# Sparse attention of the recurrent mixer: heads in the order 0, 4, 1, 5, ..., with two score products issued together over 64 rows each

## Chip, cores and metric

One NeuronCore of one Trainium2 chip runs the whole program. The metric is device microseconds from launch to end, the median of three runs. The clock that TensorE was granted is 0.998 of full speed on average.

## The reference, cut to what matters

The program is a small model of several layers on 256 tokens of width 1024. Its first layer mixes tokens in two ways side by side: a recurrent scan of eight heads (RWKV-7) and a sparse attention of eight query heads over two key/value heads (NSA). The attention is what the change touches. For each block of 128 queries it makes three softmax attentions and adds them with gates: over compressed keys, over selected keys, and over a window.

```
q = q.reshape(B, T, Hk, G, dk) * (dk ** -0.5)        # Hk = 2 key/value heads, G = 4 query heads each, dk = 64
s = jnp.einsum('bqhgd,bhcd->bhgqc', qb, k_cmp)       # compressed branch: 15 keys
s = jnp.einsum('bqhgd,bqhnjd->bhgqnj', qb, kg)       # selected branch
s = jnp.einsum('bqhgd,bkhd->bhgqk', qb, kwb)         # window branch
s = s - slopes * distance; mask; softmax; times values
return gb[..., 0:1] * o_c + gb[..., 1:2] * o_s + gb[..., 2:3] * o_w
```

All of it is float32, and the contraction of every score product is 64 long.

## The kernel before, in words

**Units.** `att_units("nsa")` (L249) lists 34 units of attention, in the order in which all engines take them. For the first 128 queries (t = 0, K = 128 keys) there are eight units of the selected branch (units 0 to 7, one for each head), one unit for the whole compressed branch (unit 8, `cmp`), and eight of the window branch (9 to 16). For the second 128 queries (t = 1, K = 256 keys) the same follows as units 17 to 24, 25 (`cmp`) and 26 to 33.

**Layout of q and k.** `qT[:, j, :]` holds, transposed, head j on rows 0 to 63 and head j + 4 on rows 64 to 127. `ksT` and `kwT` (L203) hold the keys of key/value head 0 on rows 0 to 63 of slice 0, those of head 1 on rows 64 to 127 of slice 1; the other rows of each slice are zeros (L1822). So the score product of one head runs over all 128 rows, and the zeros take out the other head.

**One step `nsa(i)`.** TensorE (L874) does three things in step i: the score product of unit i into bank `ps[3 + i % 2]` after a wait on `max_ready`, the product with values of unit i - 3 into bank 6 or 7, and the transpose of the probabilities of unit i - 2 into `ps[5]`. VectorE (L2202) adds the distance bias to the scores of unit i and takes their maximum in one custom instruction (L2217; for the compressed unit four instructions, L2211 to L2215), which counts `max_ready` up. After the last unit of a group it also normalises the group's output (`nsa_result`, L2176). ScalarE (L1468) makes the exponential of unit i - 1 and copies the transposed probabilities of unit i - 2 (L1491).

**Where the steps stand.** They are woven by hand into the block inversion of the recurrent scan, 24 rounds q = 0 to 23 (L785 on TensorE). In each round TensorE makes four products P into `ps[0]`; then the first step `nsa`, if the round has one; then it waits for ScalarE's copy of P (L1436, `P_ev`) and makes four products dM; then four transposes MT (L821, to round 20); then the second step, if there is one. VectorE's order in a round is: first step, masked copy of dM (L2133 or L2137, L2141), copy of MT (L2146), second step. `NSA_STEPS` (L231) gives the counts: none in rounds 0 and 1, one in even rounds, two in odd ones, and one in each of the last two. So a step is either "first in round" (between P and dM) or "second in round" (between MT and the next P, odd rounds 3 to 21). Up to round 11 P and dM stream 128 columns each and ScalarE copies 512 columns of P; from round 12 on it is half of both. Steps 32 to 36 stand in the tail after the rounds (L827).

**Queues.** Each engine runs its instructions in order. A wait at the head of TensorE's step holds everything behind it. Nothing of the DMA queues stands in this stretch.

Of the kernel before, what the change touches and what calls it, by code (L numbers as in the profile page):

```python
# [15 lines left out]
P = 128  # L16
# [4 lines left out]
HD = 64  # L21
# [71 lines left out]
def build(nc, x_in, wstream, gains, consts_in, masks_in, scratch, out):  # L93
    ctx = ExitStack()
    with ctx:
        at = {}

        def sb(name, shape, dt=F32):
            at[name] = nc.sbuf_base
            return ctx.enter_context(nc.sbuf_tensor(name, shape, dt))  # L100
# [16 lines left out]
        s = {n: ctx.enter_context(nc.semaphore(n)) for n in names}  # L117
# [15 lines left out]
        ps = [ctx.enter_context(nc.psum_tensor(f"ps{i}", [P, 512], F32)) for i in range(8)]  # L133

        def C(name, lo=0, hi=None):
            o, n = COL[name]
            return cst[:, o + lo:o + (n if hi is None else hi)]

        def W(off, *shape):
            n = int(np.prod(shape))  # L140
            a = wk[:, off:off + n]
            if len(shape) == 2:
                a = a.rearrange("p (a b) -> p a b", b=shape[1])
            if len(shape) == 3:
                a = a.rearrange("p (a b c) -> p a b c", b=shape[1], c=shape[2])
            return a
# [54 lines left out]
        qT = W(18432, 4, T)  # L201
# [17 lines left out]
        vsw = misc[:, 768:1280].rearrange("p (t n) -> p t n", t=TT)  # L219
        hid = sb("hid", [P, 2, 160])  # L220
        hid_k, hid_v = hid[:, :, 0:32], hid[:, :, 32:160]
        kcT = sb("kcT", [P, 2, 16])
# [5 lines left out]
        nSS, nPp, nPT = W(8192, 3, T), W(8960, 3, T), W(9728, 2, 2 * P)  # L228
# [20 lines left out]
        def att_units(kind):  # L249

            units = []
            for t in range(TT):
                K, tk = P * (t + 1), slice(t * P, (t + 1) * P)
                if kind == "nsa":
                    for n, b in enumerate(BRANCHES):
                        grp = 3 * t + n
                        if b == 0:

                            units.append(dict(cmp=True, q=[qT[:, j, tk] for j in range(4)], K=P, grp=grp, pos=0, last=True,
                                              dist=C("alibi_cmp", 16 * t, 16 * t + 16)))  # L260
                            continue
                        for h in range(8):
                            g, slope = h // 4, 2.0 ** -(h + 1)
                            kx, o = (ksT, kwT)[b - 1], (b - 1) * P + g * HD
                            units.append(dict(cmp=False, q=qT[:, h % 4, tk], scale=slope, grp=grp, pos=h, last=h == 7,
                                              k=kx[:, g, 0:K], K=K, v=[vsw[:, kt, o:o + HD] for kt in range(t + 1)],
                                              dist=C("alibi", P * (1 - t), P * (1 - t) + K)))
                if kind == "fox":
                    for h in range(8):
                        units.insert(2 * h + t, dict(  # L270
                            q=fqT[:, h // 2, tk], k=fkT[h // 4][:, h // 2 % 2, h % 2, 0:K], K=K, scale=1.0,
                            v=[evtok[:, kt, 512 + h * HD:512 + (h + 1) * HD] for kt in range(t + 1)],
                            dist=fbias[t][:, h, :]))
                if kind == "dsa":
                    for h in range(16):
                        units.append(dict(q=oqT[:, h // 2, tk], k=khT[h % 2][:, h // 2, 0:K], K=K, scale=1.0,
                                          v=[vh[kt][:, h * HD:(h + 1) * HD] for kt in range(t + 1)],
                                          t5=bias16[:, h, P * (1 - t):P * (1 - t) + K], sel=selm[:, t, 0:K]))
            return units
# [63 lines left out]
        PB = {"in": 0, "even": BLOCKS["in"], "odd": BLOCKS["in"] + BLOCKS["even"]}  # L343

        UN = {k: att_units(k) for k in ("nsa", "fox", "dsa")}
        NSA_LAST = [i for i, a in enumerate(UN["nsa"]) if a["last"]]
        RESULTS = {"fox": len(NSA_LAST), "dsa": len(NSA_LAST) + 2}
# [87 lines left out]
        def _(pe):  # L435
# [3 lines left out]
            def mm(o, l, r, start=True, stop=True):  # L439
                return pe.matmul(o, l, r, start=start, stop=stop, skip_group_check=True)  # L440
# [341 lines left out]
            def rwkv():  # L782
                pe.wait_ge(s["A_read"], RWKV_UNITS)
                i = 0
                for q in range((LEVELS - 1) * QUADS):  # L785
# [16 lines left out]
                    for _ in range(min(NSA_STEPS[q], 1)):  # L802
                        nsa(i)
                        i += 1
# [18 lines left out]
                    for _ in range(NSA_STEPS[q] - 1):  # L823
                        nsa(i)
                        i += 1
# [48 lines left out]
            def nsa(i):  # L874

                units = UN["nsa"]
                n = len(units)
                if i < n:
                    a = units[i]
                    if i >= 2:  # L880
                        pe.wait_ge(s["max_ready"], i - 1)
                    if a["cmp"]:
                        for j in range(4):
                            last = mm(ps[3 + i % 2][:, 32 * j:32 * j + 32], a["q"][j], kcT[:].rearrange("p g c -> p (g c)"))
                        last.then_inc(s["S_ps"], 1)
                    else:
                        mm(ps[3 + i % 2][:, 0:a["K"]], a["q"], a["k"]).then_inc(s["S_ps"], 1)
                if i >= 3:
                    u, a = i - 3, units[i - 3]
                    pe.wait_ge(s["npT_ev"], u + 1)  # L890
                    if u == 0:
                        pe.wait_ge(s["gate_tok"], 1)
                        pe.wait_ge(s["cmp_ready"], 1)
                    if a["pos"] == 0 and a["grp"] >= 2:
                        pe.wait_ge(s["o_ready"], a["grp"] - 1)
                    o = ps[6 + a["grp"] % 2]
                    if a["cmp"]:
                        mm(o[:, :], nPT[:, u % 2, 0:P], Vbd.rearrange("p u n -> p (u n)")).then_inc(s["o_ps"], 1)
                    else:
                        for k in range(0, a["K"], P):  # L900
                            last = mm(o[:, a["pos"] * HD:(a["pos"] + 1) * HD], nPT[:, u % 2, k:k + P],
                                      a["v"][k // P], k == 0, k + P >= a["K"])
                        last.then_inc(s["o_ps"], 1)
                if 2 <= i < n + 2:
                    u, a = i - 2, units[i - 2]
                    pe.wait_ge(s["p_ready"], u + 1)
                    for k in range(0, a["K"], P):
                        last = pe.transpose(ps[5][:, k:k + P], nPp[:, u % 3, k:k + P], ident)
                    last.then_inc(s["pT_ps"], 1)
# [977 lines left out]
        def _(v):  # L1887
            cnt = {}

            def V(ins, name="v_step"):  # L1890

                cnt[name] = cnt.get(name, 0) + 1
                ins.then_inc(s[name], 1)
                v.wait_ge(s[name], cnt[name])
# [307 lines left out]
            def nsa(i):  # L2202

                a = UN["nsa"][i]
                K = a["K"]
                v.wait_ge(s["S_ps"], i + 1)
                if i >= 3:
                    v.wait_ge(s["p_ready"], i - 2)
                if a["cmp"]:
                    z = nSS[:, i % 3, 0:P].rearrange("p (u c) -> p u c", c=16)  # L2210
                    V(v.tensor_tensor(z, ps[3 + i % 2][:, 0:P].rearrange("p (u c) -> p u c", c=16),  # L2211
                                      a["dist"].unsqueeze(1).to_broadcast([P, 8, 16]), ALU.add))
                    V(v.tensor_reduce(cmp_max, z, AX.X, ALU.max))
                    V(v.tensor_tensor(z, z, cmp_max.unsqueeze(2).to_broadcast([P, 8, 16]), ALU.subtract))
                    V(v.tensor_tensor(z, z, slopes.unsqueeze(2).to_broadcast([P, 8, 16]), ALU.mult), "max_ready")  # L2215
                else:
                    V(v.tensor_tensor_reduce(nSS[:, i % 3, 0:K], ps[3 + i % 2][:, 0:K], a["dist"], -a["scale"], 3e38,  # L2217
                                             ALU.add, ALU.min, nmax[:, i % 4:i % 4 + 1]), "max_ready")
                if i >= 2 and UN["nsa"][i - 2]["cmp"]:

                    u, g = i - 2, UN["nsa"][i - 2]["grp"] % 3
                    v.wait_ge(s["p_ready"], u + 1)
                    V(v.tensor_reduce(den[:, 8 * g:8 * g + 8], nPp[:, u % 3, 0:P].rearrange("p (u c) -> p u c", c=16),
                                      AX.X, ALU.add))
                if i - 3 in NSA_LAST:
                    nsa_result(NSA_LAST.index(i - 3))
# [451 lines left out]
```

## Time and profile before

| what | us |
|---|---|
| median of 3 runs (lowest, highest) | 1471.29 (1470.66, 1471.62) |
| the profiled execution, its time | 1470.55 |
| its span, first to last instruction | 1468.8 |
| TensorE busy in the span | 1434.4 |
| VectorE, ScalarE busy | 958.8, 698.5 |
| the stretch with the attention units, from the span's start | about 138 to 232 |

A float32 product is two passes in the trace: one product with its weight load shows as two LDWEIGHTS (PEld) and two MATMUL (PE). In a timeline equal instructions that follow each other are merged: a row gives the start, the time from the first start to the last end, and the count. A PE row ends about 0.17 us after its last pass has streamed in. Nearly all products carry line L440, that of a helper, so shapes and tile names tell them apart: `128*128` is rows by columns of the weights, `128x256` rows by columns of what streams.

### The profile page before, as it was taken

How to read it: one execution, taken by the hardware profiler on the slowest of the kernel's cores; microseconds unless marked ns; L12 is line 12 of the kernel's file. 1: busy time of each engine (PE TensorE's matmuls, PEld its weight loads, DVE VectorE, ACT ScalarE, POOL GpSimd, SP SyncE). 2: the span in 40 equal slices, each digit the busy share in tenths (PEclk: the TensorE clock that was granted, in tenths of full speed). 3: DMA queues.
4: the chain of work that ended last, by engine and by line, in shares of the span. 5: the costliest groups of instructions: out<-in, count | busy, mean ns of one | idle time of the engine just before them, and what ended most of it. 6: DMA issues, size and time to landing. Idle time of an engine off the chain costs nothing. (4 is left out here: it accounts for less than half of the span.)

```text
span 1468.8 us, 26041 instructions
## 1 busy us (share of the span) xinstructions
PE 1434.4 (98%) x10266; PEld 1320.2 (90%) x10266; DVE 958.8 (65%) x1559; ACT 698.5 (48%) x1119; POOL 86.2 (6%) x140
## 2 busy tenths in 40 slices
PE   8999999999999999999999999999999999999998
PEld 7887998899998999989989999999999878899997
DVE  4765657766667766667467666676665667576665
ACT  6753444544345434456564434353443656544342
POOL 1040001000002000010000000000000114000000
PEclk9999999999999999999999999999999999999999
DMA  9343001655553645524336545545555423365440
GB/s 348 145 152 130 1 1 44 240 201 189 176 204 127 224 171 195 191 90 169 128 113 244 203 171 198 189 158 190 200 182 183 162 86 144 145 217 196 171 172 29
DMA packets 26575, 238.06 MB, mean 162 GB/s; under 512 B 2544, under 2 KB 6784, under 8 KB 7808
## 3 DMA queue, kind: packets, MB, share of 16 engines
q1 hardware_dynamic: 23824, 233.39, 43.5%
q10 hardware_dynamic: 2672, 3.58, 0.7%
q8 instruction: 53, 0.87, 0.2%
q14 instruction: 26, 0.21, 0.0%
HBM read 235.89 MB, written 1.07 MB: 161 GB/s over the span
## 5 line engine op out<-in xcount | busy, mean ns | idle before, releaser
L440 PE MATMUL ps<-uT_h,w_gu 128*128 128x256 f32 x3520 | 614.0, 280 | 0.3 <-DVE w_gu L1952 0.2
L440 PEld LDWEIGHTS ps<-uT_h,w_gu 128*128 128x128 f32 x3520 | 537.7, 188 | 11.0 <-issue 1.4
L440 PE MATMUL ps<-uT_l,w_gu 128*128 128x256 f32 x1760 | 478.7, 279 | 0.0
L440 PE MATMUL ps<-w_dn,h_r 128*128 128x512 f32 x1320 | 326.2, 396 | 0.3 <-DVE h_r L1994 0.3
L440 PEld LDWEIGHTS ps<-uT_l,w_gu 128*128 128x128 f32 x1760 | 325.4, 188 | 0.0
L440 PEld LDWEIGHTS ps<-w_dn,h_r 128*128 128x128 f32 x1320 | 239.4, 188 | 51.2 <-issue 1.7
L1302 ACT CAST w_gu<-ring 128x2048 fp32r<-128x2048 f32 x110 | 209.9, 1909 | 155.1 <-PE ps L440 154.7
L1952 DVE TENSOR_TENSOR w_gu<-ring,w_gu 128x2048 fp32r<-128x2048 f32 x110 | 252.1, 2292 | 34.4 <-ACT w_gu L1302 34.0
L1985 DVE TENSOR_TENSOR us<-ps,bc 128x256 f32<-128x256 f32 x110 | 46.5, 423 | 202.4 <-PE ps L440 202.4
L1315 ACT ACTIVATE wk<-wk 128x256 f32<-128x256 f32 x110 | 46.2, 420 | 261.5 <-DVE wk L1983 261.4
L1308 ACT CAST w_dn<-ring 128x1024 fp32r<-128x1024 f32 x110 | 115.7, 1052 | 82.8 <-PE ps L440 82.6
L1958 DVE TENSOR_TENSOR w_dn<-ring,w_dn 128x1024 fp32r<-128x1024 f32 x110 | 134.2, 1220 | 5.3 <-ACT w_dn L1308 5.1
L440 PE MATMUL ps<-uT_h,ring_r 128*128 128x256 f32 x408 | 114.3, 281 | 0.0
L440 PE MATMUL ps<-wk 128*128 128x128 f32 (+6 forms) x624 | 95.8, 304 | 5.0 <-ACT wk L1436 2.9
L440 PEld LDWEIGHTS ps<-wk 128*128 128x128 f32 (+3 forms) x624 | 73.3, 187 | 12.7 <-ACT wk L1436 4.9
L440 PEld LDWEIGHTS ps<-uT_h,ring_r 128*128 128x128 f32 x408 | 77.5, 190 | 0.3
L1983 DVE TENSOR_TENSOR wk<-ps,bc 128x256 f32<-128x256 f32 x110 | 46.7, 425 | 37.8 <-PE ps L440 22.6
L440 PE MATMUL ps<-ring_r,uT_h 128*128 128x512 f32 (+2 forms) x176 | 62.0, 352 | 0.0
L440 PE MATMUL ps<-uT_h,in_h 128*128 128x256 f32 x176 | 50.7, 290 | 2.5 <-PE ps L440 1.2
L1988 DVE TENSOR_TENSOR wk<-wk,us 128x256 f32<-128x256 f32 x110 | 46.7, 425 | 7.7 <-ACT wk L1315 4.5
L1788 POOL TENSOR_SCALAR small<-small 128x1 f32<-128x1 f32 (+3 forms) x19 | 9.1, 480 | 688.9 <-ACT xn L1246 483.4
L1994 DVE TENSOR_TENSOR h_r<-wk,h_r 128x256 fp32r<-128x256 f32 x110 | 46.8, 425 | 3.8
(385 smaller groups left out, 1804.2 us busy)
## 6 DMA issues: line engine op xcount, KB each, us to landing
ring<-wstream SPq DMA_DIRECT2D x144, 1536.0 KB, 6.2
cst<-consts_in SPq DMA_DIRECT2D x1, 2185.0 KB, 13.8
wk<-t_row ACTq DMA_DIRECT2D x1, 2048.0 KB, 7.9
wk<-masks_in SPq DMA_DIRECT2D x1, 1216.0 KB, 24.2
x<-x_in SPq DMA_DIRECT2D x2, 512.0 KB, 4.9
ring<-wstream SPq DMA_DIRECT2D x1, 1024.0 KB, 9.0
inh<-gains ACTq DMA_DIRECT2D x2, 512.0 KB, 9.2
out_dram<-x SPq DMA_DIRECT2D x3, 256.0 KB, 2.1
```

The lines of the kernel that those rows point to most:

```text
L440: return pe.matmul(o, l, r, start=start, stop=stop, skip_group_check=True)
L1302: act.copy(w_gu[:, c % 2, 0, :], slot(i)[:, 0:2 * D]).then_inc(s["hi_a"], 1)
L1308: act.copy(w_dn[:, c % 2, 0, :], slot(i)[:, 2 * D:3 * D]).then_inc(s["hi_b"], 1)
L1315: act.activation(sg[:, c % 2, :], sg[:, c % 2, :], ACT.Silu).then_inc(s["silu_ready"], 1)
L1788: G(gp.tensor_scalar(o, i, scale, eps, ALU.mult, ALU.add))
L1952: v.tensor_tensor(w_gu[:, c % 2, 1, :], slot(i)[:, 0:2 * D], w_gu[:, c % 2, 0, :].bitcast(F32), ALU.subtract).then_inc(s["lo_a"], 1)
L1958: v.tensor_tensor(w_dn[:, c % 2, 1, :], slot(i)[:, 2 * D:3 * D], w_dn[:, c % 2, 0, :].bitcast(F32), ALU.subtract).then_inc(s["lo_b"], 1)
L1983: v.tensor_tensor(h, ps[4 + c % 2][:, 0:T], bc[:], ALU.mult).then_inc(s["gs_ready"], 1)
L1985: v.tensor_tensor(us[:], ps[6 + c % 2][:, 0:T], bc[:], ALU.mult).then_inc(s["us_ready"], 1)
L1988: v.tensor_tensor(h, h, us[:], ALU.mult).then_inc(s["h_mul"], 1)
L1994: v.tensor_tensor(hr[:, 1, :], h, hr[:, 0, :].bitcast(F32), ALU.subtract).then_inc(s["h_ready"], 1)
```

## The change

The heads of a branch are taken in the order 0, 4, 1, 5, 2, 6, 3, 7. Units get a field `second`: 0 for heads 0 to 3 (and the compressed unit), 1 for heads 4 to 7. q and k are cut to the 64 rows of their own key/value head. In the step of a unit with `second` 0 TensorE issues the score products of this unit and of the next, one on the upper 64 rows into `ps[3]`, one on the lower 64 rows into `ps[4]`. In the step of a unit with `second` 1 it issues no score product. The wait at the head of the step is now for all units before i (before: for all before i - 1). VectorE reads `ps[3 + second]`. Everything else of the step stays.

```diff
-                        for h in range(8):
+                        for n8, h in enumerate((0, 4, 1, 5, 2, 6, 3, 7)):
                             g, slope = h // 4, 2.0 ** -(h + 1)
                             kx, o = (ksT, kwT)[b - 1], (b - 1) * P + g * HD
-                            units.append(dict(cmp=False, q=qT[:, h % 4, tk], scale=slope, grp=grp, pos=h, last=h == 7,
-                                              k=kx[:, g, 0:K], K=K, v=[vsw[:, kt, o:o + HD] for kt in range(t + 1)],
+                            r = slice(g * HD, (g + 1) * HD)
+                            units.append(dict(cmp=False, q=qT[r, h % 4, tk], scale=slope, grp=grp, pos=h, last=h == 7,
+                                              second=n8 % 2, k=kx[r, g, 0:K], K=K, v=[vsw[:, kt, o:o + HD] for kt in range(t + 1)],
...
-                    if i >= 2:
-                        pe.wait_ge(s["max_ready"], i - 1)
+                    if i and not a["second"]:
+                        pe.wait_ge(s["max_ready"], i)
                     if a["cmp"]:
                         for j in range(4):
-                            last = mm(ps[3 + i % 2][:, 32 * j:32 * j + 32], a["q"][j], kcT[:].rearrange("p g c -> p (g c)"))
+                            last = mm(ps[3][:, 32 * j:32 * j + 32], a["q"][j], kcT[:].rearrange("p g c -> p (g c)"))
                         last.then_inc(s["S_ps"], 1)
-                    else:
-                        mm(ps[3 + i % 2][:, 0:a["K"]], a["q"], a["k"]).then_inc(s["S_ps"], 1)
+                    elif not a["second"]:
+                        for m in range(2):
+                            b = units[i + m]
+                            mm(ps[3 + m][:, 0:b["K"]], b["q"], b["k"]).then_inc(s["S_ps"], 1)
...
-                    V(v.tensor_tensor_reduce(nSS[:, i % 3, 0:K], ps[3 + i % 2][:, 0:K], a["dist"], -a["scale"], 3e38,
+                    V(v.tensor_tensor_reduce(nSS[:, i % 3, 0:K], ps[3 + a["second"]][:, 0:K], a["dist"], -a["scale"], 3e38,
```

The pairs start at units 0, 2, 4, 6, 9, 11, 13, 15 (K = 128) and 17, 19, 21, 23, 26, 28, 30, 32 (K = 256).

## Rows read from the trace of the kernel before

**Rows 1.** The page, part 1: busy time, share of the span, instructions.
```profile
PE 1434.4 (98%) x10266; PEld 1320.2 (90%) x10266; DVE 958.8 (65%) x1559; ACT 698.5 (48%) x1119; POOL 86.2 (6%) x140
```

**Rows 2.** Windows: span, busy us and (count) per engine, TensorE clock, DMA share, GB/s.
```profile
130.00:140.00 10.00, 8.97 (x77) 8.38 (x76) 4.17 (x10) 5.33 (x16) 0.00 (x0) 1.00 0.95 377
...
232.00:234.00 2.00, 1.22 (x10) 1.11 (x10) 1.54 (x2) 1.63 (x2) 0.39 (x1) 0.88 0.00 0
234.00:236.00 2.00, 2.00 (x12) 2.00 (x10) 1.90 (x5) 0.00 (x0) 0.00 (x0) 0.50 0.03 8
```

**Rows 3.** Timeline (start, us, engine, line, operation): six 64-row products between full-height ones.
```profile
97.66 0.28 PE L440 MATMUL ps<-in_h,uT_l 128*128 128x256 f32 x1
97.87 1.36 PE L440 MATMUL ps<-wk 64*128 64x256 f32 x12
...
99.15 0.39 PE L440 MATMUL ps<-in_h,uT_h 128*128 128x256 f32 x1
...
99.38 0.28 PE L440 MATMUL ps<-ring_r,uT_h 128*128 128x256 f32 x1
...
102.41 1.19 PEld L440 LDWEIGHTS ps<-wk 64*128 64x128 f32 x12 [0.32 <-issue]
```

**Rows 4.** Timeline of 0.01 us windows inside them: the passes in flight.
```profile
97.87 0.49 PE L440 MATMUL ps<-wk 64*128 64x256 f32 x2
97.87 0.70 PE L440 MATMUL ps<-wk 64*128 64x256 f32 x4
```

**Rows 5.** Timeline: a 24-row transpose before unit 0, and unit 0's transpose.
```profile
137.95 0.30 PE L969 MATMUL ps<-cst,ffb 24*128 24x24 f32 x2
...
143.43 0.14 PEld L908 LDWEIGHTS ps<-cst,wk 128*128 128x128 f32 x1 [0.18 <-ACT wk L1483]
```

**Rows 6.** Timeline, rounds 5 and 6, unit 6 first in round.
```profile
150.45 1.06 PE L440 MATMUL ps<-wk,xn 128*128 128x128 f32 x8
151.26 0.29 DVE L2217 CUSTOM_DVE_ANT_0 wk<-ps,cst 128x128 f32<-128x128 f32 x1
...
151.73 0.28 PE L908 MATMUL ps<-cst,wk 128*128 128x128 f32 x1
152.18 1.16 PE L440 MATMUL ps<-wk 128*128 128x128 f32 x8 [0.16 <-ACT wk L1436]
```

**Rows 7.** Timeline, round 8: bias and maximum of unit 8, dM.
```profile
159.06 0.29 DVE L2215 TENSOR_TENSOR wk<-wk,small 128x128 f32<-128x128 f32 x1
...
159.68 1.16 PE L440 MATMUL ps<-wk 128*128 128x128 f32 x8 [0.17 <-ACT wk L1436]
```

**Rows 8.** Timeline, rounds 12 and 13.
```profile
173.12 0.29 DVE L2217 CUSTOM_DVE_ANT_0 wk<-ps,cst 128x128 f32<-128x128 f32 x1
...
173.78 1.11 PE L440 MATMUL ps<-wk 128*128 128x64 f32 x8
...
175.16 1.28 PE L440 MATMUL ps<-wk 128*128 128x64 f32 x10
...
176.63 1.10 PE L440 MATMUL ps<-wk 128*128 128x64 f32 x8
```

**Rows 9.** Timeline, rounds 15 to 17.
```profile
182.47 0.65 PE L440 MATMUL ps<-wk 128*128 128x256 f32 x2
...
186.82 0.42 DVE L2217 CUSTOM_DVE_ANT_0 wk<-ps,cst 128x256 f32<-128x256 f32 x1
...
187.63 1.00 PE L440 MATMUL ps<-wk 128*128 128x64 f32 x8
...
188.91 1.49 PE L440 MATMUL ps<-wk 128*128 128x64 f32 x10
...
190.86 1.00 PE L440 MATMUL ps<-wk 128*128 128x64 f32 x8
```

**Rows 10.** Timeline, round 22: unit 29's bias and maximum, dM.
```profile
208.98 0.42 DVE L2217 CUSTOM_DVE_ANT_0 wk<-ps,cst 128x256 f32<-128x256 f32 x1
...
210.48 0.68 PE L440 MATMUL ps<-wk 128*64 128x64 f32 x8
```

More of the change, by code:

```diff
@@ L257, in att_units @@
                         if b == 0:
-                            units.append(dict(cmp=True, q=[qT[:, j, tk] for j in range(4)], K=P, grp=grp, pos=0, last=True,
+                            units.append(dict(cmp=True, second=0, q=[qT[:, j, tk] for j in range(4)], K=P, grp=grp, pos=0, last=True,
                                               dist=C("alibi_cmp", 16 * t, 16 * t + 16)))
                             continue
-                        for h in range(8):
+                        for n8, h in enumerate((0, 4, 1, 5, 2, 6, 3, 7)):
                             g, slope = h // 4, 2.0 ** -(h + 1)
                             kx, o = (ksT, kwT)[b - 1], (b - 1) * P + g * HD
-                            units.append(dict(cmp=False, q=qT[:, h % 4, tk], scale=slope, grp=grp, pos=h, last=h == 7,
-                                              k=kx[:, g, 0:K], K=K, v=[vsw[:, kt, o:o + HD] for kt in range(t + 1)],
+                            r = slice(g * HD, (g + 1) * HD)
+                            units.append(dict(cmp=False, q=qT[r, h % 4, tk], scale=slope, grp=grp, pos=h, last=h == 7,
+                                              second=n8 % 2, k=kx[r, g, 0:K], K=K, v=[vsw[:, kt, o:o + HD] for kt in range(t + 1)],
                                               dist=C("alibi", P * (1 - t), P * (1 - t) + K)))
@@ L2210, in nsa @@
                     z = nSS[:, i % 3, 0:P].rearrange("p (u c) -> p u c", c=16)
-                    V(v.tensor_tensor(z, ps[3 + i % 2][:, 0:P].rearrange("p (u c) -> p u c", c=16),
+                    V(v.tensor_tensor(z, ps[3][:, 0:P].rearrange("p (u c) -> p u c", c=16),
                                       a["dist"].unsqueeze(1).to_broadcast([P, 8, 16]), ALU.add))
```

## The prediction

> **What bounds the kernel now.** The page's busy times come first: TensorE is busy 98% of the span, VectorE and ScalarE far less [rows 1], so time is won or lost only where TensorE works or waits. Then the windows over the attention's stretch: TensorE is busy 8.97 to 10.00 of every 10 us between 130 and 230 us, at a granted clock of 1.00 (2.4 GHz), and no DMA matters [rows 2]. In so full a stretch a few tenths for each unit decide, so the rest is read from the timeline, round by round. It shows two kinds of places. Up to round 11, after the last pass of P, ScalarE's copy of P takes longer than the step that is put there: dM starts at 152.18 instead of at 151.84, where it would follow the step's last transpose (151.73 + 0.11), and with its weight load uncovered [rows 6]. From round 14 on dM follows the step without a gap, and the step itself is what takes the time [rows 9]. After 232 us TensorE waits on a chain that begins inside this stretch, and then streams the feed-forward layers with its weights at hand; so I count a microsecond lost here as lost at the end, and none of it as recovered.
>
> **What a pair costs.** A float32 product is two passes. A pass of 128 streamed columns (or 64, behind a weight load) comes every 0.11 us (eight passes of P in 1.06 us, of which the last is 0.28 long) [rows 6]. So one score product at K = 128 takes 0.22 us, and at K = 256 it takes 0.43 to 0.49 (the pass after the first comes up to 0.27 later, 0.65 less 0.38, and streams 0.22) [rows 9]. Pairs over 64 rows are already in this kernel: six products (twelve passes) of the recurrent part stand between full-height ones, at 97.87 us [rows 3]. There two passes start together at 97.87 and the next two at 98.19 [rows 4], and the last start at 98.95 (97.87 + 1.36 - 0.28): six slots, four of 0.22 and two of 0.11 less a start, for twelve passes [rows 3]. So two 64-row products do run side by side, in the time of one: 0.22 us at 256 columns for two passes, 0.11 at 128. A pair at K = 128 would stream in 0.22 us, at K = 256 in 0.43.
>
> Going over to 64 rows and back has a price. The full-height pass of 97.66 takes 0.12, so the next could start at 97.78; it starts at 97.87, with its weight load uncovered: the second two come 0.10 late (0.32 behind the first instead of 0.22). At the end the last two passes start at 98.95, last 0.11, and the full-height pass starts at 99.15 instead of 99.06; it is 0.39 long instead of 0.28, with its uncovered load in it, and the one behind it comes 0.11 late (99.38, not 99.27) [rows 3, 4]. Together 0.09 + 0.10 + 0.09 + 0.11 = 0.39 us for one visit. For a lone pair I take the same. Below, the price could be nothing, if the loads run ahead where the neighbours are float32 too; above, 0.62: ahead of the next such entry, at 102.41, the loads were idle for 0.32 with nothing to wait for [rows 3], and that can stand in place of the 0.09. So in the same place a pair costs 0.22 + 0.39 = 0.61 against 0.22 at K = 128, **0.39 more**, and 0.82 against 0.43 to 0.49 at K = 256, **0.35 more**. The step of its second unit is then 0.22 or 0.43 shorter. That is a loss of 0.17 for each pair at K = 128 and a gain of some 0.1 at K = 256, before any wait; which of the two is felt depends on the place.
>
> The Trainium skill, "TensorEngine Tiling (Array Packing)", section "Theoretical Speedup", gives up to twice the speed where a dimension is 64 or less. The rows agree for the streaming alone. By it the pairs would save 5.2 us in all, the second rival's sum below; by the rows most of that goes back into the visits.
>
> **Pairs with nothing to hide behind.** Units 11, 17, 23 and 26 are second in round, 32 stands in the tail between two groups of products. TensorE goes straight on after them: 0.39 + 4 x 0.35 = **+1.8**. Unit 0 stands behind a 24-row transpose, where a change of height is paid already: only half comes on top, **+0.2**. Unit 2 is followed by a transpose that waits for ScalarE's first exponential, which hides some: **+0.1** [rows 5]. Units 4 and 13 are first in odd rounds up to 11. From P's end to an undelayed dM pass there are 0.96 us (150.45 + 0.88 = 151.33 to 152.18 + 0.10 for the uncovered load) and the step with a pair takes 0.52 + 0.39 = 0.91: **0**.
>
> **Pairs that must wait for VectorE.** The new wait is for the unit before, not the one before that. Where that unit is second in the previous round, VectorE reads it only after its copies of dM and MT. Queued behind the wait are the value product and the transpose of the same step and then dM, and all of the round hangs on dM.
> - Unit 6 (round 6): TensorE would be there at 151.1; unit 5 is read until 151.55 [rows 6]. The pair starts at 151.60, its visit ends at 152.01 (0.21 + 0.11 + 0.09), value product with uncovered load 0.28, transpose 0.11: dM could follow at 152.40, against an undelayed 152.28. **+0.1**.
> - Unit 9 (round 8): the compressed unit's four instructions end at 159.35 [rows 7]. From 159.40 the same 0.80 gives 160.20, against 159.68 + 0.10: **+0.4**.
> - Unit 15 (round 12): unit 14 is read until 173.42 [rows 8]; 173.47 + 0.80 = 174.27 against 173.78 + 0.11: **+0.4**.
> - Units 19 and 21 (rounds 15, 16): VectorE is late here, since it normalises a group in round 15, and that chain starts from unit 19's scores, which come 0.22 later in a pair. Unit 20 is read until 187.24 [rows 9], so 187.46. The pair starts at 187.51, its visit takes 0.31 + 0.22 + 0.09, the value product (four passes, uncovered load) 0.50, two transposes 0.22: dM at 188.85 against 187.63. **+1.2**, with unit 19's own visit and unit 20's missing product in it.
> - Units 28 and 30 (rounds 21, 22): the same with the compressed group's result. Unit 29 is read until 209.40 [rows 10], 0.38 later with the visit of unit 28: the pair starts at 209.83, 1.34 later comes 211.17, and dM of 64-column weights 0.09 after it at 211.26, against 210.48. **+0.8**.
>
> Together **+2.9**. The wait alone, were the visits free, would cost 0.2 + 0.2 + 0.8 + 0.2 = 1.4 of that (units 9, 15, 21, 30, each worked out as above with 0.22 or 0.43 for the pair and one uncovered load).
>
> **Steps that lose their product.** Units 1, 3, 7, 10, 12 and 16 stand behind P where ScalarE's copy is the bound already: 0. Units 5, 14, 20 and 29 stand ahead of a pair that waits for VectorE: swallowed, and counted above. Units 22, 24, 27 and 31 are first in rounds where dM follows without a gap. In round 17 P ends at 189.79 and dM starts at 190.86, 1.07 later [rows 9]. ScalarE's copy becomes the bound then: in round 13, where it bounds, an undelayed dM would start 0.69 after P's end (175.16 + 0.88 to 176.63 + 0.10) [rows 8]. So 0.38 is won, of the 0.43 removed. Four of these, two of them a little more (the 64-column dM): **-1.6**. Unit 18 gives 0.1, unit 33 in the tail 0.15: **-0.25**.
>
> **Sum.** 1.8 + 0.2 + 0.1 + 2.9 - 1.6 - 0.25 = +3.2 us on the profiled execution's own 1470.55 (span 1468.8 and 1.75 around it), so 1473.7; that execution lies 0.74 under the median of the runs, and on the median it is **1474.5**. The other parts of the change cost nothing: the same VectorE and ScalarE instructions run on the same shapes, and the compressed unit's bank is free by the same wait. One bound: with visits free the sum is 1.4 - 1.85 = -0.45, so some 9.5 visits of 0.39 are felt in it; at 0.62 it is +5.4.
>
> **Rivals.**
> - *A visit between float32 neighbours is cheap* (the other side: not slower). The sum is -0.45 plus 9.5 times the price of a visit. It decides from 0.35 us: below it the change is within 0.2%, at 0.05 it is nought. For it: the rows' 0.39 are from six products and fp32r or wide neighbours. Against it: the gap and the uncovered load show on both sides. Time 1471 to 1474, middle 1472.3. Chance 0.30.
> - *The pairs count at face value*, all 8 x 0.22 + 8 x 0.43 = 5.2 us, since TensorE is busy 98% and the waits fall into slack that I misread: 1466.1. Against it: the gap ahead of dM in [rows 6] and the times at which VectorE reads unit 5, 14, 20. Chance 0.05.
> - *The pairs don't run side by side*, since each is two lone products with their own increments: up to 5.2 us more of streaming, some of it under ScalarE's copies, so 1478.5. Against it: the two passes at 97.87. Chance 0.06.
> - *The clock falls once inside the stretch.* After 0.8 us of waiting within 2 us the granted clock went to 0.88, 0.50 (1.2 GHz) over the next four [rows 2]; the new waits are 0.3 to 0.9 us each. The same again loses 2 x 0.12 + 2 x 0.50 = 1.2 us: 1475.7. Against it: 130 to 140 us had 1.03 us idle and kept 1.00. Chance 0.09.
>
> **How the numbers follow.** My forecast has the chance 0.50, its own range 1473.3 to 1475.9. A change of under 0.2%, 2.9 us, can't be told from none. That cuts the forecast's own range: 0.36 of it is slower, 0.14 within. With the rivals: slower 0.36 + 0.06 + 0.08 = 0.50; same 0.14 + 0.27 + 0.01 = 0.42; faster 0.05 + 0.03 = 0.08. The range reaches from visits nearly free (1470.8) to pairs hardly overlapping (1477.9).
>
> **What would show it.** Right: 64-row passes in twos at 16 places between 138 and 217 us; an uncovered weight load at each, on entry and on leaving; TensorE idle ahead of the pairs of rounds 6, 8, 12, 16 and 22, released by VectorE's L2217 (or L2215), the longest in round 16; the gap ahead of dM in round 17 ended by ScalarE's L1436; and the recurrent part's last products at 214.5 some 3 us later. Wrong: that point earlier than before, visits under 0.3 us, or a clock under 1.00 between 138 and 230 us.

## The result, and the profile after

| | before | after |
|---|---|---|
| median of 14 runs, us (lowest, highest) | 1471.03 (1470.34, 1472.40) | 1474.32 (1473.69, 1475.18) |
| ratio of the medians, 95% interval | | 1.0023 (1.0016 to 1.0030) |
| the profiled execution: its time, its span | 1470.55, 1468.8 | 1474.35, 1472.5 |

The change makes the kernel slower by 3.3 us, 0.2%. The forecast was 1474.5 us, and slower. In the later series two executions of the kernel before took 4992.63 and 2588.10 us; they are left out of the ratios.

First the page of the kernel after: TensorE's busy time has hardly moved (1434.4 before, 1434.2 after [rows 1]), though 32 score products were halved in height. The span is 3.7 us longer, so what came in is idle time of TensorE, and some 1.4 us of the time before are products at a lower clock (below).

```profile
PE 1434.2 (97%) x10266; PEld 1315.2 (89%) x10266; DVE 958.4 (65%) x1559; ACT 698.6 (47%) x1119; POOL 86.5 (6%) x140
```

The windows agree. Between 130 and 140 us TensorE is busy 8.97 us as before [rows 2]; from 180 to 190 us it was busy 9.22 us of 10, and 10.00 before. The granted clock (the column before the DMA share) stayed at 1.00, the upper level of 2.4 GHz.

```profile
130.00:140.00 10.00, 8.97 (x77) 8.26 (x76) 4.08 (x10) 5.64 (x17) 0.00 (x0) 1.00 0.91 359
...
180.00:190.00 10.00, 9.22 (x78) 7.99 (x76) 6.74 (x17) 4.03 (x14) 0.00 (x0) 1.00 0.01 2
...
236.00:238.00 2.00, 1.22 (x12) 1.11 (x12) 1.50 (x2) 1.63 (x2) 0.43 (x1) 1.00 0.00 0
238.00:240.00 2.00, 2.00 (x21) 2.00 (x20) 1.90 (x5) 0.00 (x0) 0.00 (x0) 1.00 0.03 8
```

To compare executions that reach the attention at slightly different times, I measure one **stretch** in each timeline: from the start of the gates' 24-row transposes to the start of the value product of step 34. These are its ends after the change, and below them its end before (its start before is in [rows 5]).

```profile
138.54 0.30 PE L972 MATMUL ps<-cst,ffb 24*128 24x24 f32 x2
...
229.60 0.61 PE L441 MATMUL ps<-misc,wk 128*128 128x64 f32 x4
```

```profile
225.56 0.61 PE L440 MATMUL ps<-misc,wk 128*128 128x64 f32 x4
```

The stretch took 87.61 us before and takes 91.06 after: **+3.45 us**. The two spans differ by 3.7; the execution after had reached the stretch 0.59 later than the one before, and 0.34 came back behind it.

The 0.34 is not the change's. Behind the stretch both kernels have the same wait, with TensorE busy 1.22 us of 2. Before, the granted clock then fell to 0.88 and 0.50 [rows 2]; after, it stayed at 1.00 (the last two windows above). From that wait's end to the first product of 512 columns TensorE took 7.32 us before (233.26 to 240.58) and 5.93 after (237.30 to 243.23). Behind those slow products VectorE had to stand idle for 0.46 us before, and not after. The first row is from before, the second from after:

```profile
238.87 0.69 DVE L2326 TENSOR_TENSOR uT_l<-ps,uT_h 128x512 fp32r<-128x512 f32 x1 [0.46 <-ACT uT_h L1534]
```

```profile
242.49 0.69 DVE L2329 TENSOR_TENSOR uT_l<-ps,uT_h 128x512 fp32r<-128x512 f32 x1
```

These two rows lie 3.62 us apart; the same rows of VectorE ahead of the fall (232.42 and 236.46) lie 4.04 apart, which is 0.59 + 3.45. So 0.42 us come from the clock; 0.08 us of other differences follow further on. TensorE, which won 1.4 us there, gives most of it back in a wait for VectorE (0.8 us, the row of L2329 below). So the whole of the change lies in the stretch.

The waits after (who waited for whom, us in total, times, longest) show three releasers that were not among TensorE's before: VectorE's L2220 (L2217 before) and L2218 (L2215 before) inside the stretch, and L2329 (L2326 before) behind it.

```profile
PE ps L441 <- DVE small L2220: 2.1, 4, 0.8
...
PE ps L441 <- DVE uT_l L2329: 0.8, 1, 0.8
...
PE ps L441 <- DVE wk L2218: 0.4, 1, 0.4
```

The four of L2220 and the one of L2218 make the five steps that were named: units 6, 15, 21, 30, and unit 9. Here are the timelines that answer to [rows 6 to 10]. Rounds 5 and 6, unit 6:

```profile
151.14 1.06 PE L441 MATMUL ps<-wk,xn 128*128 128x128 f32 x8
...
152.18 0.29 DVE L2220 CUSTOM_DVE_ANT_0 wk<-ps,cst 128x128 f32<-128x128 f32 x1
...
152.63 0.49 PE L441 MATMUL ps<-wk 64*128 64x128 f32 x4 [0.43 <-DVE small L2220]
...
153.05 0.43 PE L441 MATMUL ps<-misc,wk 128*128 128x64 f32 x2
...
153.44 1.06 PE L441 MATMUL ps<-wk 128*128 128x128 f32 x8
```

Read it in order. P ends at 152.02 (151.14 and eight passes of 0.11). VectorE is still at unit 5 until 152.47, and the pair starts at 152.63 instead of the 152.52 that I had allowed. Its visit ends with the value product at 153.05, 0.42 later: 0.22 of streaming, and the rest the way in and out. That product is 0.43 long for two passes where it was 0.33, with its weight load in it; and dM, which before stood 0.16 idle ahead of its first pass [rows 6], now follows back to back. Round 8, unit 9 behind the compressed unit:

```profile
160.22 0.29 DVE L2218 TENSOR_TENSOR wk<-wk,small 128x128 f32<-128x128 f32 x1
...
160.57 0.49 PE L441 MATMUL ps<-wk 64*128 64x128 f32 x4 [0.40 <-DVE wk L2218]
...
161.38 1.06 PE L441 MATMUL ps<-wk 128*128 128x128 f32 x8
```

Rounds 12 and 13. Unit 15 waits in the first; in the second TensorE waits for ScalarE's copy as before (dM is 1.10 long, its load uncovered):

```profile
175.12 0.29 DVE L2220 CUSTOM_DVE_ANT_0 wk<-ps,cst 128x128 f32<-128x128 f32 x1
...
175.47 0.49 PE L441 MATMUL ps<-wk 64*128 64x128 f32 x4 [0.39 <-DVE small L2220]
...
176.28 1.00 PE L441 MATMUL ps<-wk 128*128 128x64 f32 x8
...
179.03 1.10 PE L441 MATMUL ps<-wk 128*128 128x64 f32 x8
```

Rounds 15 to 17. The pair of unit 21 has TensorE's longest wait in this stretch, 0.85 us, for VectorE's reading of unit 20, which stands behind the group's normalisation and two copies. In round 17 unit 22 has no product: from P's end (192.82 + 0.88) to dM there are 0.64 us (0.70 to an undelayed pass) where there were 1.07 [rows 9], and ScalarE's copy of P (its row is the L1439) is what ends them.

```profile
185.31 0.70 PE L441 MATMUL ps<-wk 64*128 64x256 f32 x4
...
189.70 0.42 DVE L2220 CUSTOM_DVE_ANT_0 wk<-ps,cst 128x256 f32<-128x256 f32 x1
...
190.19 0.70 PE L441 MATMUL ps<-wk 64*128 64x256 f32 x4 [0.85 <-DVE small L2220]
...
191.54 1.00 PE L441 MATMUL ps<-wk 128*128 128x64 f32 x8
...
192.82 1.00 PE L441 MATMUL ps<-wk 128*128 128x64 f32 x8
...
193.87 0.37 ACT L1439 COPY wk<-ps 128x256 f32<-128x256 f32 x1 [1.75 <-PE ps L441]
...
194.34 1.06 PE L441 MATMUL ps<-wk 128*128 128x64 f32 x8
```

Round 22, unit 30 behind unit 29:

```profile
212.84 0.42 DVE L2220 CUSTOM_DVE_ANT_0 wk<-ps,cst 128x256 f32<-128x256 f32 x1
...
213.33 0.70 PE L441 MATMUL ps<-wk 64*128 64x256 f32 x4 [0.45 <-DVE small L2220]
...
214.77 0.68 PE L441 MATMUL ps<-wk 128*64 128x64 f32 x8
```

One landmark of each round gives the whole account: the start of its transposes MT (from round 21 on, of dM, and in the tail of the products there), taken from the stretch's start, after less before. Each entry is what this round adds.

| round | what stands there | forecast | measured |
|---|---|---|---|
| 2 | unit 0's pair | +0.2 | +0.20 |
| 4 | unit 2's pair (second in 3) | +0.1 | +0.12 |
| 5, 11 | pairs of 4 and 13, behind P | 0 | +0.01, +0.01 |
| 6 | unit 6 waits | +0.1 | +0.24 |
| 8 | unit 9 waits | +0.4 | +0.44 |
| 10 | unit 11's pair (second in 9) | +0.39 | +0.39 |
| 12 | unit 15 waits | +0.4 | +0.41 |
| 14 | unit 17's pair (second in 13), 18 without | +0.35 - 0.1 | +0.36 |
| 15, 16 | 19's pair, 20 without, 21 waits | +1.2 | +0.33 + 0.82 |
| 17 | unit 22 without | -0.38 | -0.38 |
| 18 | 23's pair (second in 17), 24 without | +0.35 - 0.38 | +0.02 |
| 20 | 26's pair (second in 19), 27 without | +0.35 - 0.4 | -0.03 |
| 21, 22 | 28's pair, 29 without, 30 waits | +0.8 | +0.34 + 0.43 |
| 23 | unit 31 without | -0.4 | -0.43 |
| tail | 32's pair, 33 without | +0.35 - 0.15 | +0.34 - 0.16 |

### The profile page after: what moved, and what is told of

It reads as the page before. It is cut to its first block and busy times, and to the rows that moved or that the text cites. A ratio compares the mean times of both kernels' runs of the same rounds, so it can differ in the third digit from the quotient of the medians.

```text
span 1472.5 us, 26041 instructions
## 1 busy us (share of the span) xinstructions
PE 1434.2 (97%) x10266; PEld 1315.2 (89%) x10266; DVE 958.4 (65%) x1559; ACT 698.6 (47%) x1119; POOL 86.5 (6%) x140
## 3 DMA queue, kind: packets, MB, share of 16 engines
HBM read 235.89 MB, written 1.07 MB: 161 GB/s over the span
## 5 line engine op out<-in xcount | busy, mean ns | idle before, releaser
L441 PE MATMUL ps<-wk 128*128 128x128 f32 (+6 forms) x624 | 90.3, 308 | 8.2 <-ACT wk L1439 3.3
L441 PEld LDWEIGHTS ps<-wk 128*128 128x128 f32 (+3 forms) x624 | 69.5, 187 | 17.4 <-issue 5.4
```

## The experiments

The forecast came true, but a sum can come true by terms that are wrong together. Its three parts are the visits to 64 rows, the new wait, and the streaming saved. Four kernels take them apart, and two more try to gain from what they show; the four were timed against the kernel before (median 1470.90 us in that series).

**Pairs over 128 rows.** From the changed kernel: the same order, pairs and waits, but the operands at full height.

```diff
-units.append(dict(cmp=False, q=qT[r, h % 4, tk], ..., second=n8 % 2, k=kx[r, g, 0:K], ...
+units.append(dict(cmp=False, q=qT[:, h % 4, tk], ..., second=n8 % 2, k=kx[:, g, 0:K], ...
```

Expected: 

> The changed kernel with its order, its pairs and its waits, but q and k over all 128 rows again (zeros on the other half), so no product goes over to 64 rows. Marks: the stretch from the 24-row transposes of the gates to the value product of step 34, 87.61 us before, 91.06 after the change (+3.45). My account (visits and waits cost, side-by-side streaming saves as much): the visits' 0.35 to 0.39 go, 0.22 (K = 128) or 0.43 (K = 256) of streaming comes in their place at each pair that is felt. By rounds: units 0 to 16 +1.6, units 17 to 33 +2.2, so the stretch is +3.8 us on before, 0.3 to 0.6 slower than the change. Rival, visits cost much and the streaming nothing: +0.5. Rival, the 64-row streaming is what gains and visits cost little: this one is +5 or more.

Measured: 1474.93 us, ratio 1.0028 (1.0017 to 1.0038). The stretch took 91.56 us, +3.95 on before (138.02 to 229.58), of it +1.6 up to round 12 and the rest after. The first row shows a pair at K = 256 in round 13: four passes one behind the other, the last starting 0.65 after the first.

```profile
179.66 1.03 PE L441 MATMUL ps<-wk 128*128 128x256 f32 x4
...
180.53 0.33 PE L441 MATMUL ps<-misc,wk 128*128 128x64 f32 x2
```

The value product follows 0.87 after the pair's start, with its load covered (0.33 long). At 64 rows a pair takes 0.63 (190.19 to 190.82), with the way in and the uncovered load still to add. So all that the half height brings to pairs is half a microsecond in the whole stretch, 3.95 against 3.45: at K = 128 (round 10) the 64-row pair costs 0.39 where this one costs 0.21, at K = 256 (round 15) 0.33 where this one costs 0.43.

**Single products over 64 rows.** From the kernel before: its order, its steps, its wait, but each product over its own 64 rows.

```diff
-units.append(dict(cmp=False, q=qT[:, h % 4, tk], ..., k=kx[:, g, 0:K], ...
+r = slice(g * HD, (g + 1) * HD)
+units.append(dict(cmp=False, q=qT[r, h % 4, tk], ..., k=kx[r, g, 0:K], ...
```

Expected: 

> The kernel before with its order, one product a step and its old wait, but each of the 32 score products over its own 64 rows. So it has a visit for each unit, nothing side by side, and no new wait. My account: 0.35 to 0.39 at each unit where TensorE goes straight on (5, 11, 14, 17 to 24, 26 to 32), 0.2 at units 0, 15, 16 and 33, nothing behind ScalarE's copy (1, 3, 4, 6, 7, 9, 10, 12, 13): 1.9 + 5.5 = +7.4 us. Rival, a visit is cheap between float32 products and the waits made the change slower: under +2. In the trace: each unit's 64-row product with its load uncovered, and the value product after it too.

Measured: the stretch took 94.86 us (139.20 to 234.06), **+7.25** for an expected 7.4. By rounds: nothing in 5, 7 to 9 and 11, +0.39 in 6 (unit 5, the second of round 5), +0.38 in 10, +0.32 to 0.37 for each unit where TensorE goes straight on at K = 256 (+0.32, +0.73, +0.33, +0.72 in rounds 15 to 18, each with the 1, 2, 1 and 2 units since the landmark before). So a visit has its price for a lone product between float32 neighbours too, and the rival that had it cheap is out. A single product of 64 rows in round 15, and the value product behind it, 0.63 later and with its load in it:

```profile
186.34 0.70 PE L441 MATMUL ps<-wk 64*128 64x256 f32 x2
186.97 0.43 PE L441 MATMUL ps<-misc,wk 128*128 128x64 f32 x2
```

Set beside unit 21's pair above: two products side by side are 0.70 long, one alone is 0.70 long. The second product of a pair streams for free; that was the half of the forecast that rested on [rows 4].

The time of this kernel was 1480.77 us, ratio 1.0070 (1.0057 to 1.0082), more than the stretch gives. Its six runs fall in two groups: three at 1478.7 to 1479.2 with a mean clock of 0.998 to 0.999 (the profiled one among them), three at 1482.4 to 1482.7 with 0.995. The sizes here are therefore taken from the stretch.

**The wait alone.** From the kernel before: nothing but the wait, at the steps where the change has it.

```diff
 if i >= 2:
-    pe.wait_ge(s["max_ready"], i - 1)
+    first = i in (0, 2, 4, 6, 8, 9, 11, 13, 15, 17, 19, 21, 23, 25, 26, 28, 30, 32)
+    pe.wait_ge(s["max_ready"], i if first else i - 1)
```

Expected: 

> The kernel before, with full-height single products in its old order, and only the change's wait (all units before i read) at the steps where the change has it: the compressed units and each first of a pair. My account: 0 at unit 6, 0.2 at units 9, 15 and 30, 0.8 at unit 21, so +1.4 us. Rival, the wait alone makes the change's whole loss: +3. Rival, the wait falls into slack: 0.

Measured: 1472.29 us, ratio 1.0010 (1.0001 to 1.0019). The stretch took 89.12 us (138.50 to 227.62), **+1.51**: 0.24 in round 8, 0.21 in round 12, 0.83 in round 16, 0.23 in round 22, and at most 0.01 in any other. Unit 21 again:

```profile
188.31 0.70 PE L440 MATMUL ps<-wk 128*128 128x256 f32 x2 [0.61 <-DVE small L2218]
```

**VectorE reads the second unit early.** From the changed kernel: in rounds 5, 11, 15 and 21 VectorE takes the second step's unit right after the first's, ahead of its copies.

```diff
 for _ in range(min(NSA_STEPS[q], 1)):
     nsa(i)
     i += 1
+if NSA_STEPS[q] == 2 and i in (5, 14, 20, 29):
+    nsa(i)
...
 for _ in range(NSA_STEPS[q] - 1):
-    nsa(i)
+    if i not in (5, 14, 20, 29):
+        nsa(i)
     i += 1
```

Expected: 

> The changed kernel, but VectorE takes units 5, 14, 20 and 29 right behind units 4, 13, 19 and 28, ahead of its copies of dM and MT of the same round (their scores lie there since the pair was issued). The pairs of units 6, 15, 21 and 30 then need not wait for it; only unit 9 waits, for the compressed unit. My account: round 6 goes from +0.24 to -0.2, round 12 from +0.40 to 0, rounds 15 and 16 from +1.16 to +0.3, round 22 from +0.77 to +0.3: the stretch at +1.2 us on before instead of +3.45. Rival, the waits are only where a delay shows and the visits are the whole cost: still +3 or more. Rival, VectorE's copies of dM, now 0.3 to 0.4 us later, hold the next round's dM: +2 to +3.

Measured: 1472.49 us, ratio 1.0010 (1.0001 to 1.0019). The stretch took 88.76 us (138.22 to 226.98), **+1.15** for an expected 1.2. Round 6 adds -0.22, round 12 -0.06, rounds 15 and 16 +0.33 and -0.09; unit 9's +0.44 stays. In round 16, P and the pair are one block of twelve passes now, with no wait between them, and unit 20 was read (187.24 to 187.66) before the copy of dM:

```profile
187.08 1.64 PE L441 MATMUL ps<-wk 128*128 128x64 f32 x12
...
187.24 0.42 DVE L2223 CUSTOM_DVE_ANT_0 wk<-ps,cst 128x256 f32<-128x256 f32 x1
...
187.71 0.44 DVE L2142 COPY_PREDICATED wk<-msk,ps 128x256 f32<-128x256 uint8 x1
```

In the stretch two thirds of the change's loss go by an order on another engine, with every visit kept (by the medians about half: +1.6 us against +3.3, and the interval of the 1.6 reaches from 0.1 to 2.8). What is left, 1.15 us, is visits less removed products, and unit 9.

**Fewer visits.** If the price belongs to the visit and the streaming is saved by the pair, four products a visit should pay at K = 256. This kernel leaves the first 128 queries as before. For the second 128 it issues units 17 to 20, 21 to 24, 26 to 29 and 30 to 33 together, one in each half of banks 3 and 4; VectorE waits for all four before it reads the first, and takes units 20 and 29 early.

```diff
+for i in (17, 21, 26, 30):
+    units[i]["issue"], units[i]["need"] = [i, i + 1, i + 2, i + 3], i
+    for m in range(4):
+        units[i + m]["slot"], units[i + m]["seen"] = (3 + m % 2, 256 * (m // 2)), i + 4
+        if m:
+            units[i + m]["issue"] = []
...
+if a["need"] > 0 and a["issue"]:
+    pe.wait_ge(s["max_ready"], a["need"])
...
+for m in a["issue"]:
+    b = units[m]
+    bank, lo = b["slot"]
+    mm(ps[bank][:, lo:lo + b["K"]], b["q"], b["k"]).then_inc(s["S_ps"], 1)
...
-v.wait_ge(s["S_ps"], i + 1)
+v.wait_ge(s["S_ps"], a["seen"])
```

Expected: 

> A version that should pay: the kernel before for the first 128 queries (single products over 128 rows, the old wait); for the second 128 queries four score products in one visit to 64 rows (units 17 to 20, 21 to 24, 26 to 29, 30 to 33), two in each half of banks 3 and 4, VectorE waiting for all four, and taking units 20 and 29 ahead of the dM copy, so that the visits at 21 and 30 need not wait. My account: a visit with four costs 1.25 us where one product took 0.45, four times +0.8; the twelve steps without product give 0.43 or what ScalarE's copy leaves (0.38), 0.1 at unit 18, 0.3 and 0.15 in the tail, in all -4.3. The stretch at -1.1 us on before. Rival, going back and forth costs more with both halves of two banks in use or VectorE becomes late: 0 or slower. Rival, side-by-side streaming is worth its face value, 0.43 a product: -3.5.

Measured: 1470.91 us against 1470.80 in this series, ratio 1.0000 (0.9991 to 1.0009). The stretch took 87.01 us (137.79 to 224.80), **-0.60** where I expected -1.1. One visit with four products, in round 13, from the first pass to the value product takes 1.06 us:

```profile
177.94 1.14 PE L451 MATMUL ps<-wk 64*128 64x256 f32 x8
179.00 0.43 PE L451 MATMUL ps<-misc,wk 128*128 128x64 f32 x2
```

By rounds it adds +0.78 (14), -0.16 (15), +0.34 (16), -0.37 (17), -0.81 (18), +0.40 (20), -0.43 (21), +0.42 (22), -0.44 (23) and -0.32 in the tail. The visits are as sized. I had over-counted what the steps without a product give. In round 15 it is 0.16, not 0.38, since unit 16's value product and so the room between P's end and dM is shorter there than in round 17: 0.84 (181.63 + 0.88 to 183.35, below) against 1.07, and by the prediction's 0.69 dM can't come earlier. Unit 18 gave nothing for 0.1, and the tail 0.32 for 0.45. Round 15 of the kernel before:

```profile
181.63 1.00 PE L440 MATMUL ps<-wk,uT 128*128 128x64 f32 x8
...
183.35 1.00 PE L440 MATMUL ps<-wk 128*128 128x64 f32 x8
```

**Pairs where there is room.** The former, and for the first 128 queries pairs of units 1 and 2, 4 and 5, 10 and 11, 13 and 14, each issued behind P in an odd round, heads in the order 0, 1, 5, 2, 3, 7, 4, 6.

```diff
+for i in (1, 4, 10, 13):
+    units[i]["issue"], units[i]["need"], units[i + 1]["issue"] = [i, i + 1], i, []
...
```

Expected: 

> The former, and in the first 128 queries pairs over 64 rows only where the round has room: units 1 and 2, 4 and 5, 10 and 11, 13 and 14, issued first in an odd round behind P, where ScalarE's copy of P is the bound (0.91 us of work in 0.96), so that the second in round (5, 11, 14) loses its product. Heads go 0, 1, 5, 2, 3, 7, 4, 6 there. My account: 3 x 0.22 = 0.66 less than the former, the stretch at -1.8 us on before, the time at some 1469.2. Rival, the pairs there are felt as elsewhere: as the former or slower.

Measured: 1470.23 us against 1470.80, ratio 0.9995 (0.9986 to 1.0004). The stretch took 86.34 us (139.26 to 225.60), **-1.27** where I expected -1.8 (and a time of some 1469.2 us). It is 0.67 less than the former, for an expected 0.66, so the miss is the former's. Rounds 6, 10 and 12 add -0.21, -0.22 and -0.23, and the rounds with the pairs in them nothing. Round 5: the pair's visit ends with a value product at 149.48 and dM follows at 149.87, while ScalarE's copy would have held it until then anyway.

```profile
149.48 0.43 PE L453 MATMUL ps<-misc,wk 128*128 128x64 f32 x2
...
149.87 1.09 PE L453 MATMUL ps<-wk 128*128 128x128 f32 x8
```

It is the best of the versions, 4 us under the change, and its trace is 1.3 us shorter in this stretch than the kernel before; the times alone can't tell it from before.

## Why the prediction was right

- **TensorE goes straight from a step to dM or P.** Right, and the reason why tenths of a microsecond could be added up: the shifts of the table appear in the named rounds and in no other.
- **The price of a visit.** Right: 0.39 at K = 128 (round 10) and 0.33 to 0.36 at K = 256, from a block of six products at another place of the program. The single products confirmed it with +7.25 us for 32 visits, of which nine cost nothing behind ScalarE's copy.
- **Pairs run side by side.** Right; one product alone and two together are both 0.70 long. The rival of 1478.5 us is out.
- **The wait takes the place of the product removed.** Right in place and nearly in size: alone it costs 1.51 us for a forecast of 1.4. In unit 6 the two together were +0.24 for +0.1: TensorE took up the pair 0.16 after VectorE's row ended, not the 0.05 that I had allowed (in rounds 12 and 22 it was 0.06 and 0.07), and the visit and the load behind it took the rest. Why it was later in round 6 no run shows.
- **The removed product gives only what ScalarE's copy leaves.** Right where it was read from the trace (0.38 in round 17 for 0.38). It failed for unit 18, which I had at 0.1: rounds 13 and 14 together gave the whole +0.36 of unit 17's visit and nothing back. The same step, carried over by eye to round 15 of the kernel with four products a visit, was 0.2 off.
- **The sum.** 3.2 us forecast, 3.45 in the stretch, 3.3 between the medians. It is no luck: term by term the table is off by at most 0.14 us, and the errors at units 6 and 18 add up instead of cancelling. The recurrent part's last products came at 218.34 us for 214.48, 3.27 later counted from the stretch's start. The 1474.5 us were counted from a median of three runs, 1471.29, that lay 0.26 above the one of 14. That a microsecond lost in the stretch is lost at the end held too: the kernel with pairs over 128 rows, whose trace has the same fall of the clock behind the stretch as before, is 4.02 us behind at the stretch's end and 4.0 in its span.
- **The clock.** It stayed at 1.00 in the stretch, with 0.85 us of waiting at once; that rival is out for the change. The rows that it was taken from don't carry it either: the same 0.78 us of waiting stands before 237.30 us in the trace of the change, and there the clock stayed at 1.00. For the single products over 64 rows there is no trace of the slower group: see below.

The Trainium skill's "TensorEngine Tiling (Array Packing)", section "Theoretical Speedup", has up to twice the speed for a dimension of 64. For the streaming of a pair the runs agree: 0.70 us for two as for one. As a forecast of this change it would have had the wrong sign.

## What to carry to other kernels

Halving the height of a product saved nothing by itself here: price the way into and out of the smaller tile from a place of the trace where it already happens, and ask how many products share one visit (against full height, two at 128 columns lost 0.18 us and two at 256 gained 0.10; four at 256 shortened the stretch). When two buffers are filled at once, the wait moves by one consumer: look at what stands between the last reader's turn and its work on the reading engine, since an order there may win back more than the idea was worth. Put such pairs where another engine's copy is the bound already, so that the visit is hidden and the step freed elsewhere is not.

## What the runs showed of the hardware that I had not expected

- The kernel with all 32 score products alone over 64 rows came in two groups of times, 1478.7 to 1479.2 us at a mean granted clock of 0.998 to 0.999 and 1482.4 to 1482.7 at 0.995, three runs each. All 14 runs of the change were at 0.998 or 0.999. A mean of 0.003 less over 1480 us is about 4.4 us of the clock's full level, and 3.7 us were lost. The profiled execution was of the first group, so where the clock fell stays open, and whether the 64-row products have to do with it too.
- The fall of the clock at 232 to 238 us before, which cost TensorE 1.4 us and VectorE's chain 0.42, stands in two of the eight traces (before, and pairs over 128 rows, at 236 to 242 us), not in the other six, though all have the wait of 0.78 us ahead of it. Runs at a mean clock of 0.998 were 0.4 us longer than runs at 0.999, both for the change (1474.48 and 1474.08 us, seven each) and for the kernel before in the first later series (1471.16 and 1470.77). That agrees with the 0.42 but does not show that it is this fall; the kernel with four products a visit has it the other way (three runs against eight).
- The kernel with four products a visit had a stretch 0.60 us shorter than before and an unchanged median, its runs spread from 1469.48 to 1471.47. With differences of under 1 us the landmarks of one trace were sharper than 11 timed runs: in rounds that no edit touched they repeat within 0.01 us. They say nothing of what lies outside the stretch.
- Where full-height and 64-row products meet, the first weight load of either kind stays uncovered, 0.10 to 0.11 us each (value product 0.43 us behind a visit, 0.33 behind a full-height pair), and a gap of some 0.09 us lies ahead of it (97.78 to 97.87 us of the kernel before [rows 3]). So half of the visit's price is the load that no longer runs ahead.
